# The head norms of the third layer: from column sums and turned scales to a block matrix in two fp32r passes

## The reference, cut to what matters

```python
def rmsnorm_2(x, g):
    x32 = x.astype(jnp.float32)
    y = x32 * lax.rsqrt(jnp.mean(x32 * x32, axis=-1, keepdims=True) + EPS)
    return (y * g.astype(jnp.float32)).astype(x.dtype)
...
q = rope_2(rmsnorm_2(q.reshape(b, s, N_HEADS, HEAD_DIM), q_norm_g[l]), positions)
k_sel = rope_2(rmsnorm_2(ksl.reshape(kv_shape), k_norm_g[l, 1]), positions)
k_win = rope_2(rmsnorm_2(kwn.reshape(kv_shape), k_norm_g[l, 2]), positions)
```

## Time and profile before

| | us |
|---|---|
| median of 3 runs | 1865.19 (1863.39 to 1865.94) |
| the profiled execution's own time | 1863.88 |
| its span, first to last instruction | 1862.1 |
| PE busy | 1836.1 (99%) |
| DVE busy | 855.2 (46%) |
| ACT busy | 769.0 (41%) |
| POOL busy | 1050.8 (56%) |

### The profile page before, as it was taken

One profiled execution on the slowest core, in us unless ns is written; L12 is line 12 of the kernel. 1 busy time (PEld: TensorE's weight loads), 2 busy tenths in 40 slices (PEclk: granted clock), 3 DMA queues, 4 the chain that ended last, 5 costly groups with the idle time before them and its releaser, 6 DMA issues.

```text
span 1862.1 us, 26749 instructions
## 1 busy us (share of the span) xinstructions
PE 1836.1 (99%) x9071; PEld 1517.1 (81%) x9071; DVE 855.2 (46%) x1737; ACT 769.0 (41%) x1373; POOL 1050.8 (56%) x1436
## 2 busy tenths in 40 slices
PE   9999999999999999999999999999999999999999
PEld 6876888888888877888888888887788888888887
DVE  7786532222326684322223673787742354444200
ACT  6666542323134674423232453747642342323221
POOL 6862555555546864555555564555565555555553
PEclk9999999999999999999999999999999999999999
DMA  6330233232323212332323222221123223323332
GB/s 226 117 105 1 64 101 102 91 102 90 102 91 101 70 46 70 108 102 91 102 90 101 91 91 91 75 73 35 35 91 102 91 91 101 101 90 94 109 103 78
DMA packets 47582, 168.30 MB, mean 90 GB/s; under 512 B 5632, under 2 KB 5888, under 8 KB 47232
## 3 DMA queue, kind: packets, MB, share of 16 engines
q1 hardware_dynamic: 46512, 164.64, 27.4%
q10 hardware_dynamic: 976, 2.39, 0.5%
HBM read 164.13 MB, written 2.10 MB: 89 GB/s over the span
## 4 chain that ended last, share of the span: by engine, by line
PE 92%; POOL 3%; issue 2%; DVE 2%; ACT 1%; POOLq 0%; ACTq 0%; DVEq 0%
PE bank L722 28%; PE bank L723 27%; PE bank L724 27%; PE bank L814 3%; POOL WL L630 3%; PE bank L854 2%; PE bank L865 2%; PE bank L832 1%; PE bank L827 0%; ACT PROB L1200 0%; PE bank L765 0%; PE bank L1009 0%; DVE PROB L1672 0%; PE bank L1054 0%; PE bank L1026 0%
## 5 line engine op out<-in xcount | busy, mean ns | idle before, releaser
L630 POOL TENSOR_TENSOR WL<-RAW,WH 128x256 fp32r<-128x256 f32 x1208 | 937.2, 808 | 668.6 <-ACT WH L1129 660.7
L722 PE MATMUL bank<-XH,WH 128*128 128x512 f32 x1311 | 520.8, 397 | 1.7 <-DVE KMV L1941 1.5
L724 PE MATMUL bank<-XH,WL 128*128 128x512 f32 x1311 | 510.8, 390 | 0.0
L723 PE MATMUL bank<-XL,WH 128*128 128x512 f32 x1311 | 510.7, 390 | 0.0
L1129 ACT ACTIVATE WH<-RAW 128x1024 fp32r<-128x1024 f32 x301 | 316.0, 1052 | 297.0 <-PE bank L724 293.7
L724 PEld LDWEIGHTS bank<-XH,WL 128*128 128x128 f32 x1311 | 246.1, 188 | 52.1
L722 PEld LDWEIGHTS bank<-XH,WH 128*128 128x128 f32 x1311 | 246.4, 188 | 49.7 <-DVE KMV L1941 1.7
L723 PEld LDWEIGHTS bank<-XL,WH 128*128 128x128 f32 x1311 | 246.6, 188 | 46.3
L722 PE MATMUL bank<-HH,WH 128*128 128x512 f32 x512 | 199.2, 389 | 0.0
L723 PE MATMUL bank<-HL,WH 128*128 128x512 f32 x512 | 199.2, 389 | 0.0
L724 PE MATMUL bank<-HH,WL 128*128 128x512 f32 x512 | 199.2, 389 | 0.0
(11 more groups left out here) (385 smaller groups left out, 2788.0 us busy)
## 6 DMA issues: line engine op xcount, KB each, us to landing
RAW<-stream SPq DMA_DIRECT2D x301, 512.0 KB, 3.4
out<-X SPq DMA_DIRECT2D x8, 256.0 KB, 4.6
X<-x SPq DMA_DIRECT2D x3, 512.0 KB, 8.5
MEM<-mem SPq DMA_DIRECT2D x1, 1024.0 KB, 10.5
W<-cmp_w ACTq DMA_DIRECT2D x1, 1024.0 KB, 4.6
KT<-KR ACTq DMA_DIRECT2D x1, 768.0 KB, 7.6
CT<-consts SPq DMA_DIRECT2D x1, 513.5 KB, 11.0
X<-x SPq DMA_DIRECT2D x2, 256.0 KB, 4.0
```

The source lines that it names most:

```text
L630: ins = pool.tensor_tensor(WL[:, slot, c], RAW[:, slot, c], WH[:, slot, c].bitcast(F32), ALU.subtract)
L722: pe.matmul(dst, lhs[0], rhs[0], start=start, stop=False)
L723: pe.matmul(dst, lhs[0], rhs[1], start=False, stop=False)
L724: return pe.matmul(dst, lhs[1], rhs[0], start=False, stop=stop)
```

## The change

The squares are taken as before, and ACT then writes their fp32r rounding, `hi`; DVE subtracts for `lo`. PE multiplies a 128 x 128 matrix with 1/64 inside each head's 64 x 64 block (HEAD_MEAN, written once) with `hi` and with `lo`, so bank 6 or 7 has each head's mean on all of that head's rows. ACT takes the logarithm of mean plus EPS and the exponential of minus half of it, into SBUF, and DVE's norm reads it there. The steps sum, spread, var, std, scale on DVE and widen are gone, and the tables are written anew. The new squares 2 to 5 stand behind later outputs, and the buffers for squares, halves and scales lie in TMP, ACC, WIDE (a row more) and in parts of QN that are not yet filled. SUMS and MEAN are declared and not used. The line numbers above are those of the kernel before.

```diff
+        with ExitStack() as summed:
+            SUMS = tensor(summed, "SUMS", [P, 4, S], F32R)
...
+        EPSC = tensor(ctx, "EPSC", [P, 1])
+        MEAN = tensor(ctx, "MEAN", [P, 2], F32R)
...
-                    WIDE = tensor(head_scales, "WIDE", [P, 2, S])
+                    WIDE = tensor(head_scales, "WIDE", [P, 3, S])
...
-        PE_AFTER = {3: [("sum", 0)], 4: [("sum", 1), ("sum", 2)], 5: [("sum", 3)], 6: [("sum", 4), ("spread", 0)],
-                    7: [("sum", 5), ("spread", 1)], 8: [("spread", 2)], 9: [("compress", 1), ("spread", 3)],
-                    11: [("spread", 4)], 12: [("compress", 2), ("spread", 5)], 15: [("compress", 3)],
+        PE_AFTER = {4: [("mean", 0)], 5: [("mean", 1)], 7: [("mean", 2)], 8: [("mean", 3)], 9: [("compress", 1)],
+                    10: [("mean", 4)], 11: [("mean", 5)], 12: [("compress", 2)], 15: [("compress", 3)],
                     18: [("cmp_scores", 0)]}
-        ACT_AFTER = {2: [("square", 0)], 3: [("square", 1), ("square", 2)], 4: [("square", 3), ("std", 0)],
-                     5: [("square", 4), ("widen", 0), ("widen", 1)], 6: [("square", 5), ("widen", 2)],
-                     7: [("rotate", 0), ("std", 1), ("widen", 3)], 8: [("rotate", 1)],
-                     9: [("rotate", 2), ("split", 0), ("widen", 4)], 10: [("ya", 0), ("rotate", 3), ("widen", 5)],
-                     11: [("cmp_silu", 0), ("split", 1)], 12: [("rotate", 4)], 13: [("ya", 1), ("split", 2)],
+        ACT_AFTER = {2: [("square", 0)], 3: [("square", 1)], 5: [("square", 2), ("scale", 0)],
+                     6: [("square", 3), ("scale", 1)], 7: [("rotate", 0)], 8: [("scale", 2), ("rotate", 1), ("square", 4)],
+                     9: [("scale", 3), ("rotate", 2), ("split", 0), ("square", 5)], 10: [("ya", 0), ("rotate", 3)],
+                     11: [("scale", 4), ("cmp_silu", 0), ("split", 1)], 12: [("scale", 5), ("rotate", 4)], 13: [("ya", 1), ("split", 2)],
                      14: [("rotate", 5)], 15: [("split", 3)], 16: [("ya", 2), ("split", 4), ("cmp_std", 0)],
                      17: [("split", 5)], 19: [("ya", 3), ("cmp_exp", 0)]}
-        DVE_AFTER = {4: [("var", 0), ("scale", 0)], 6: [("norm", 0)], 7: [("norm", 1), ("var", 1)],
-                     8: [("scale", 1), ("rotated", 0), ("norm", 2)], 9: [("rotated", 1), ("norm", 3)],
-                     10: [("split_lo", 0), ("cmp_bias", 0)], 11: [("ya_lo", 0), ("rotated", 2), ("norm", 4)],
+        DVE_AFTER = {2: [("square_lo", 0)], 3: [("square_lo", 1)], 5: [("square_lo", 2)], 6: [("square_lo", 3), ("norm", 0)],
+                     7: [("norm", 1)], 8: [("square_lo", 4), ("rotated", 0), ("norm", 2)],
+                     9: [("rotated", 1), ("norm", 3), ("square_lo", 5)], 10: [("split_lo", 0), ("cmp_bias", 0)], 11: [("ya_lo", 0), ("rotated", 2), ("norm", 4)],
                      13: [("cmp_rows", 0), ("rotated", 3), ("norm", 5)], 14: [("ya_lo", 1), ("rotated", 4), ("split_lo", 1)],
                      15: [("split_lo", 2)], 16: [("rotated", 5), ("cmp_var", 0)],
                      17: [("ya_lo", 2), ("cmp_keys", 0), ("split_lo", 3), ("split_lo", 4)],
                      19: [("split_lo", 5), ("cmp_softmax", 0), ("ya_lo", 3)]}
+        HEAD_MEAN = QN[:, 3, 0:P]
+
+        def head_squares(j):
+
+            return (TMP[:, 1, :] if j in (1, 3) else ACC[:]), QN[:, 4 + j % 2, :], QN[:, 6 + j % 2, :]
+
+        HEAD_SCALE = [WIDE[:, 0, :], WIDE[:, 1, :], WIDE[:, 0, :], WIDE[:, 1, :], ACC[:], WIDE[:, 2, :]]
+
         IN2_OUTS = list(range(CHANNELS + 12)) + [LAST_V]
 
...
-            def head_sum(j):
-                pe.wait_ge(signal("head_squares"), j + 1)
-                squares = (ACC, SQ)[j % 2]
-                for b in range(NT):
-                    at = b * NH + 2 * j
-                    ins = pe.matmul(BANK[6 - j // 3][:, at:at + 2], squares[:, blk(b)], const("head_rows", 0, 2), start=True,
-                                    stop=True)
-                ins.then_inc(signal("head_sums"), 1)
-
-            def head_spread(j):
-                pe.wait_ge(signal("head_scales_wide"), j + 1)
+            def head_mean(j):
+                pe.wait_ge(signal("head_squares_lo"), j + 1)
                 if j >= 2:
-                    pe.wait_ge(signal("head_normed"), j - 1)
-                for b in range(NT):
-                    ins = pe.transpose(BANK[6 + j % 2][:, blk(b)], WIDE[:, j % 2, blk(b)], IDENT)
-                ins.then_inc(signal("head_spread"), 1)
+                    pe.wait_ge(signal("head_scales"), j - 1)
+                _, hi, lo = head_squares(j)
+                pe.matmul(BANK[6 + j % 2][:], HEAD_MEAN, hi, start=True, stop=False)
+                pe.matmul(BANK[6 + j % 2][:], HEAD_MEAN, lo, start=False, stop=True).then_inc(signal("head_means"), 1)
...
             def head_square(j):
+                squares, hi, _ = head_squares(j)
                 act.wait_ge(drained, in2 + j + 1)
                 if j >= 2:
-                    act.wait_ge(signal("head_sums"), j - 1)
+                    act.wait_ge(signal("head_means"), j - 1)
+                if j == 5:
+                    act.wait_ge(signal("head_squares_lo"), 5)
                 elif j == 0:
                     act.wait_ge(scale_done, NORM_NO["norm1"] + 1)
-                act.activation((ACC, SQ)[j % 2][:], R32[:, j, :], ACT.Square).then_inc(signal("head_squares"), 1)
-
-            def head_std(g):
-                act.wait_ge(signal("head_var"), g + 1)
-                act.activation(HS[:, :, 6 * g:6 * g + 6], HS[:, :, 6 * g:6 * g + 6], ACT.Sqrt
-                               ).then_inc(signal("head_std"), 1)
-
-            def head_widen(j):
-                act.wait_ge(signal("head_scales"), j // 3 + 1)
-                if j >= 2:
-                    act.wait_ge(signal("head_spread"), j - 1)
-                act.activation(WIDE[:, j % 2, :].rearrange("p (b h n) -> p b h n", b=NT, h=2),
-                               HS[:, :, 2 * j:2 * j + 2].unsqueeze(3).to_broadcast([P, NT, 2, HD]), ACT.Copy
-                               ).then_inc(signal("head_scales_wide"), 1)
+                    act.activation(HEAD_MEAN.rearrange("p (h n) -> p h n", h=2),
+                                   const("head_rows", 0, 2).unsqueeze(2).to_broadcast([P, 2, HD]), ACT.Copy, scale=1.0 / HD)
+                own.then(act.activation(squares, R32[:, j, :], ACT.Square))
+                act.activation(hi, squares, ACT.Copy).then_inc(signal("head_squares"), 1)
+
+            def head_scale(j):
+                act.wait_ge(signal("head_means"), j + 1)
+                if j in (2, 3):
+                    act.wait_ge(signal("head_normed"), j - 1)
+                elif j == 4:
+                    act.wait_ge(signal("head_squares_lo"), 6)
+                own.then(act.activation(HEAD_SCALE[j], BANK[6 + j % 2][:], ACT.Ln, bias=EPSC[:]))
+                act.activation(HEAD_SCALE[j], HEAD_SCALE[j], ACT.Exp, scale=-0.5).then_inc(signal("head_scales"), 1)
 
             def head_rotate(j):
...
-                        act.wait_ge(signal("head_spread"), 6)
+                        act.wait_ge(signal("head_means"), 6)
+                        act.wait_ge(signal("head_normed"), 4)
+                    elif j == 3:
+                        act.wait_ge(signal("head_normed"), 6)
                     split_q((signal("head_done"), j + 1), R32[:, j, :], QN[:, 2 * (j - 2):2 * (j - 1), :])
 
...
             in0, memo = plan.out0["in0"], plan.out0["mem"]
+            dve.memset(EPSC[:], EPS)
...
-            def head_var(g):
-                dve.wait_ge(signal("head_sums"), 3 * g + 3)
-                heads = slice(6 * g, 6 * g + 6)
-                dve.tensor_scalar(HS[:, :, heads],
-                                  BANK[6 - g][:, 0:NT * NH].rearrange("p (b h) -> p b h", h=NH)[:, :, heads], 1.0 / HD, EPS,
-                                  ALU.mult, ALU.add).then_inc(signal("head_var"), 1)
-
-            def head_scale(g):
-                heads = slice(6 * g, 6 * g + 6)
-                dve.wait_ge(signal("head_std"), g + 1)
-                dve.reciprocal(HS[:, :, heads], HS[:, :, heads]).then_inc(signal("head_scales"), 1)
+            def head_square_lo(j):
+                squares, hi, lo = head_squares(j)
+                dve.wait_ge(signal("head_squares"), j + 1)
+                dve.tensor_tensor(lo, squares, hi.bitcast(F32), ALU.subtract).then_inc(signal("head_squares_lo"), 1)
 
             def head_norm(j):
-                dve.wait_ge(signal("head_spread"), j + 1)
+                dve.wait_ge(signal("head_scales"), j + 1)
                 if j >= 2:
                     dve.wait_ge(signal("head_done"), j - 1)
+                elif j == 1:
+                    dve.wait_ge(signal("head_squares_lo"), 4)
                 dve.scalar_tensor_tensor(TMP[:, j % 2, :], R32[:, j, :], gain(("k_sel", "k_win", "q")[min(j, 2)]),
-                                         BANK[6 + j % 2][:], ALU.mult, ALU.mult).then_inc(signal("head_normed"), 1)
```

(10 more changed lines are left out.)

## The result

| | before | after |
|---|---|---|
| median of 13 runs each | 1864.10 us | 1867.67 us (1865.15 to 1870.51) |
| profiled execution, own time | 1863.88 | 1866.62 |
| span | 1862.1 | 1864.7 |

The ratio is 1.0019 [1.0012, 1.0026]: 3.6 us slower, where 5.0 us faster was forecast and 1863.5 us was the upper end of the range. The sign is wrong.

The account below looks back on a forecast made before the run. PE, busy 99% of the span, was taken as the bound, with DVE as tight in part of the stage. -8.07 + 2.72 + 0.36 = -4.99 us took the median from 1865.19 to 1860.2 us, range 1858.4 to 1863.5.

Parts of the forecast that it names:

- PE, removed and added: PE's sums and spreads go, 8.07 us; six pairs of fp32r passes come, 2.72 us; net 5.35 us saved before output 13.
- Rival 4: On PE, the new passes run at the fp32 pace, 5.7 us for six; gain falls to 2 us, 1863; chance 0.03.
- DVE, the operations: Six subtractions add about 5 us, mostly hidden in DVE's waits; only norm 5 adds to the path, 0.36 us.
- ACT, "new are a load for Ln at output 5 and one at output 12": On ACT, only two new table loads of 1.28 us; outputs 8 to 12 take 32.5 us of 34.7, tight but fitting.
- rival 2: On ACT, Ln and Exp lie in two tables, about nine more loads; gain 3 to 5 us, 1861 to 1862; chance 0.06.
- What a wait of PE costs: Lateness counted at its length, as in rival 3: 9 us late less 5 is 4 us slower; no term for clock.
- After output 13: From output 13 to the stage's end, all starts 5.35 us earlier, less 0.36 us for norm 5, and the lead stays.
- Rival 1: DVE reaches output 13's drain 2 to 4 us late and swallows the lead; gain 1 to 3 us, 1862 to 1864; chance 0.14.
- Rival 3: ACT overloaded at outputs 8 to 12 by doubled loads of double length; 4 us slower, 1869; chance 0.03.
- Nothing: EPSC's memset (0 to 0.1 us), unused tensors, other addresses and HEAD_MEAN's copy ahead of the stage cost nothing; no DMA moves.

Follow-up runs that it names:

- e1: Changed kernel with one table set holding both Ln and Exp, loaded before scale 0 and after Silu, 2 loads for 12: 1861.31 us, ratio 0.9985.
- e4: Changed kernel with Ln and Exp replaced by Copy, so no table is loaded and the head norm's scale is not computed: 1859.87 us, ratio 0.9979.
- e5: Kernel before, with two copies on ACT (5.57 us) ahead of Silu and no part of the change: 1868.44 us, ratio 1.0023.
- e9: e1 with DVE's rotated 3 moved from behind output 13 to behind output 12: 1859.28 us, ratio 0.9974.
- e7: e2 (paired loads kept) with DVE's split_lo(1) moved from behind output 14 to behind output 17: 1863.96 us, ratio 0.9998.
- e10: e2 (paired loads kept) with DVE's rotated 3 moved from behind output 13 to behind output 12: 1866.23 us, ratio 1.0007.
- e2: Changed kernel with paired loads kept and Silu placed before scale 4 on ACT: 1865.45 us, ratio 1.0007.
- e3: Changed kernel with PE's scores on the compressed keys moved from behind output 18 to behind output 19: 1865.39 us, ratio 1.0007.
- e6: e1 with DVE's split_lo(1) moved from behind output 14 to behind output 17: 1862.08 us, ratio 0.9987.
- e8: Kernel before, with only DVE's split_lo(1) moved from behind output 14 to behind output 17: 1866.71 us, ratio 1.0011.

## Why the prediction was wrong, by its steps

- **PE, removed and added: right.** The passes start 0.22 us apart at full clock, and a group with one mean stands 5.89 us behind the last, 24 products and two passes. Timeline of PE:

```profile
1137.52 0.39 PE L1018 MATMUL bank<-QN 128*128 128x512 f32 x1
1137.74 0.39 PE L1019 MATMUL bank<-QN 128*128 128x512 f32 x1
...
1143.41 0.39 PE L1018 MATMUL bank<-QN 128*128 128x512 f32 x1
```

  In e1 and e4 output 13 is drained 75.65 us behind the start of the stage, where the kernel before has 81.00 (1199.70 less 1118.70): the 5.35 us of the forecast, whole. Rival 4 is out.
- **DVE, the operations: right in size.** The six subtractions take 0.69 us (four) and 1.08 us (two), 5.0 us in all; norm 5 takes 1.05 instead of 0.75 us, 0.30 more where 0.36 was counted. Subtraction 4 waited 4.22 us for ACT, not 0.7: square 4 is queued behind scale 2 with its two loads. PE did not feel it.
- **ACT, "new are a load for Ln at output 5 and one at output 12": the step that failed.** There are twelve, and with them a scale takes 3.9 us instead of 1.3. Hence "scale 4, load, Silu end at 1185.0 us, 2.9 us before PE's second compression step wants it" became 1189.64, while PE was there at 1187.74, as forecast (1187.9): the 1.96 us of the wait, with 0.06 between. The rule that I named beside rival 2 (the Trainium skill, ScalarE: Activation LUTs, Table sets: the hidden batching unit), one load for Ln and Exp, is not borne out by this kernel as it was compiled; a set with both exists, and e1 uses it with two loads. On the price of a load the records stay with the earlier trace rows: 1.28 us, the activation 0.02 us after it.
- **Rival 2 had the mechanism and the wrong price.** I carried its nine loads to rotate 4 and scale 5, and did not carry them to Silu, in the same queue and with the least time to spare. The two of scale 4 stand right before it and alone make 1185.0 into 1187.6, level with the 1187.9 of PE's need; the pairs of scales 2 and 3 further up the queue, where ACT had but one gap of 1.40 us left from 1156.8 on, do the rest.
- **What a wait of PE costs: priced at its own length.** No step had the granted clock, which was 1.00 in all stretches read the earlier trace rows. Behind these waits it was at half: 1.7 us lost after 1.96 us (2.44 us in e5), 3.4 us after 1.75 us. This turned a gain of about 1.6 us (5.35 - 1.96 - 1.75) into a loss.
- **After output 13, "the lead passes whole": it failed here and holds in e4 and e9.** DVE drained output 13 1.95 us earlier than before, and KB was only 0.18 us earlier (0.25 us of both is the earlier start of the stage in this profile): from the one to the other 28.62 us, where the kernel before has 26.85, e4 27.12 and e1 27.85. POOL caught up in this stretch; before, it ran 3.71 and 8.34 us with a gap between them, after, it ran on end (timeline of POOL, tiles in one group):

```profile
1200.99 18.14 POOL L639 TENSOR_TENSOR WL<-RAW,WH 128x256 fp32r<-128x256 f32 x16 [4.81 <-ACT WH L1130]
```

  Beside it DVE's operations of two SBUF inputs take 1.1 to 1.2 us, alone 0.69. In e4 POOL has its gap again (4.66 and 8.37 us of work). That fits a POOL that is late because ACT's WH is late behind the loads, but it was not isolated.
- **Rival 1** (DVE late at output 13) did not occur in the changed kernel, where DVE waited 4.93 us there; its mechanism is in e7 and e10. **Rival 3**'s sign was right by another way: it needed loads of double length and 5 us of lateness at norm 5. **Nothing**: right behind the stage, where nothing is gained or lost, but not quite ahead of it. Near 45 us PE waits 1.31 us for DVE's ACC in the changed kernel and 0.89 in the kernel before, and from PE's first group with a 128x1 result (near 26 us) to its second are 19.7 us in seven of the nine profiles with the change (in the other two the clock fell near 10 us, and they have 18.3 and 19.0) and 19.3 us in all four without. These 0.4 us were put at 0 to 0.1; which part of the change brings them was not tested.

**Open.** Why the clock falls behind some waits only. It did behind waits of 0.99 to 2.44 us at Silu and KB (after, e1, e2, e3, e5, e10), not behind 0.3 us at KB (before, e4), nor within the windows behind the waits for WL of 1.3 to 3.1 us (e3, e6, e7, e8). The same wait can go either way: between 695 and 700 us, far from the change, PE waits 1.9 us for the same step of ACT in both kernels, and the clock is 1.00 there in the profile before and 0.66 in the one after. Nor does a fall always cost its share: before, PE waits another 0.73 and 0.49 us right behind that place, after, it does not, and from 73 to 763 us the two profiles take 690.04 and 690.18 us. And the medians of e6 and e7 stand 1.9 and 2.0 us above what their stages say. In their profiles the stage begins 1.4 and 1.7 us later than before, so part of it is lost ahead of the stage; over all profiles it begins between 1117.77 and 1120.40 us, and why it does was not followed up.

## What to carry to other kernels

When an edit adds functions on ACT, count a load for every change of function until the trace or the compiled program shows fewer, and carry every added microsecond to each step behind it in that queue, first to the one with the least to spare. Where PE is the bound, a wait of 1 to 2.5 us can cost well over its length (2.44 us cost 4.1 in e5, where the clock behind it was at half for 3.4 us). Where two engines run level, look for a gap that the other can give before counting on a lead: e1 kept the lead in some executions only, e9 kept it by moving one step of DVE into a gap, and with the paired loads (e10) that move is worth nothing.

## What was not expected of the hardware

- The clock at 1.2 GHz right behind a single wait of PE of 0.99 us (e1) to 2.44 us (e5), for 3.4 us behind Silu and some 7 to 10 us behind KB.
- Two SBUF-input operations of DVE at 1.22 us beside POOL (the rows had 1.11), against 0.69 alone; the same operation on a bank took 0.69 in both. With that the norm from SBUF costs 0.75 to 1.22 us, mean 0.92, against 0.747 from the bank.
